# One attention kind's scores from half-height products, and a projection on rows that are normalised afterwards

## The reference, cut to what matters

```python
h = rmsnorm(x, norm1_g)                 # x * rsqrt(mean(x*x) + eps) * g, per token
proj = h @ w_in                         # 1024 x 1792, cut into aq ak av bq bk bv cu
# first kind: 4 heads, a 2-D neighbourhood, scores + relative bias, softmax, times values
# second kind: 8 query heads, 2 key/value heads, blocks of 128 queries, 3 blocks of keys
s = einsum('bnqgrd,bnkgd->bngrqk', qb, kb)      # d is 64
s = where(valid, s + alibi, -inf)               # softmax with a sink logit, times values
# third mixer: centred means over windows of 2, 4, 8, 16 tokens of cu, then a small product
x = x + concatenate([o_a, o_b, o_c]) @ w_out
# then rmsnorm, a router over 32 experts, two experts per token, and a last rmsnorm
```

## Time and profile before

| | |
|---|---|
| median of 3 runs | 747.9 us (746.43 to 748.84) |
| the profiled execution, its own time | 746.88 us |
| its span, first to last instruction | 745.0 us |
| TensorE busy | 707.8 us (95%), mean granted clock 0.986 |
| VectorE busy | 506.3 us (68%) |
| ScalarE busy | 411.1 us (55%) |
| GpSimd busy | 328.3 us (44%) |

### The profile page before, as it was taken

One profiled execution on the slowest core, in us unless ns is written; L12 is line 12 of the kernel. 1 busy time (PEld: TensorE's weight loads), 2 busy tenths in 40 slices (PEclk: granted clock), 3 DMA queues, 4 the chain that ended last, 5 costly groups with the idle time before them and its releaser, 6 DMA issues.

```text
span 745.0 us, 10230 instructions
## 1 busy us (share of the span) xinstructions
PE 707.8 (95%) x3745; PEld 522.7 (70%) x3745; DVE 506.3 (68%) x790; ACT 411.1 (55%) x619; POOL 328.3 (44%) x243
## 2 busy tenths in 40 slices
PE   6999999998898999999999899999999999999973
PEld 6888888886666665888889866666666666666631
DVE  5561110325788888613477798888888888888977
ACT  6411002224678887301122478888888888887815
POOL 3523347853578885340010144444444444443223
PEclk9999999999899999999999899999999999999998
DMA  8521111100021000915547399999999999999978
GB/s 288 154 58 58 28 57 58 56 1 1 1 58 58 0 2 1 306 34 197 187 157 255 113 347 383 381 381 382 383 387 383 390 386 382 382 386 382 393 276 342
DMA packets 62563, 157.80 MB, mean 212 GB/s; under 512 B 10184, under 2 KB 25136, under 8 KB 62512
## 3 DMA queue, kind: packets, MB, share of 16 engines
q1 hardware_dynamic: 56032, 139.72, 51.9%
q0 software_dynamic: 6336, 16.89, 6.8%
q10 hardware_dynamic: 144, 0.52, 0.2%
HBM read 142.43 MB, written 18.87 MB: 216 GB/s over the span
## 4 chain that ended last, share of the span: by engine, by line
PE 82%; DVE 6%; ACT 3%; DMA 3%; POOL 2%; issue 2%; SPq 0%; DVEq 0%; POOLq 0%
PE ps L999 8%; PE ps L1004 8%; PE ps L1007 8%; PE ps L727 6%; PE ps L728 6%; PE ps L726 6%; PE ps L882 4%; PE ps L1030 4%; PE ps L1026 4%; PE ps L884 4%; PE ps L883 4%; PE ps L1034 4%; PE ps L975 2%; POOL pswa L2030 2%; PE ps L909 2%
## 5 line engine op out<-in xcount | busy, mean ns | idle before, releaser
L1800 DVE TENSOR_TENSOR wgulo<-wgu,unit 128x2048 fp32r<-128x2048 f32 x64 | 146.3, 2287 | 27.1 <-ACT unit L1293 26.7
L1293 ACT CAST unit<-wgu 128x2048 fp32r<-128x2048 f32 x64 | 122.2, 1910 | 4.3 <-PE ps L940 2.0
L2079 POOL DMA_INDIRECT expert_rows<-ysb,idx x32 | 72.2, 2258 | 106.9 <-ACT ysb L1340 99.2
L2072 POOL DMA_INDIRECT xg<-h_rows,idx x32 | 58.8, 1839 | 73.6 <-PE ps L975 59.1
L726 PE MATMUL ps<-hThi,whi 128*128 128x512 f32 x208 | 81.4, 392 | 0.0
L728 PE MATMUL ps<-hThi,wlo 128*128 128x512 f32 x208 | 81.0, 389 | 0.0
L727 PE MATMUL ps<-hTlo,whi 128*128 128x512 f32 x208 | 80.9, 389 | 0.0
L1806 DVE TENSOR_TENSOR wdlo<-wd,unit 128x2048 fp32r<-128x2048 f32 x32 | 73.1, 2284 | 1.8 <-ACT unit L1302 1.8
L999 PE MATMUL ps<-unit,xThi 128*80 128x512 f32 x256 | 70.9, 398 | 0.8 <-ACT xThi L1317 0.8
L1004 PE MATMUL ps<-unit,xTlo 128*80 128x512 f32 x256 | 69.2, 391 | 0.0
L1007 PE MATMUL ps<-wgulo,xThi 128*80 128x512 f32 x256 | 69.1, 391 | 0.0
(11 more groups left out here) (221 smaller groups left out, 1472.9 us busy)
## 6 DMA issues: line engine op xcount, KB each, us to landing
wgu<-in_expert_w_gate SPq DMA_DIRECT2D x64, 512.0 KB, 13.0
wgu<-in_expert_w_up SPq DMA_DIRECT2D x64, 512.0 KB, 14.9
wd<-in_expert_w_down SPq DMA_DIRECT2D x32, 1024.0 KB, 16.7
y<-expert_rows SPq DMA_DIRECT2D x16, 512.0 KB, 9.9
wraw<-in_w_in SPq DMA_DIRECT2D x14, 512.0 KB, 4.0
xin<-in_x SPq DMA_DIRECT2D x8, 512.0 KB, 5.1
x<-in_x SPq DMA_DIRECT2D x8, 512.0 KB, 7.1
out<-fo SPq DMA_DIRECT2D x8, 512.0 KB, 4.1
```

Source lines behind the costliest of these rows:

```text
L1293: nc.scalar.copy(weight_unit(e, a)[:], raw_half(wgu, e, a)).then_inc(ahi_done, 1)
L1800: nc.vector.tensor_tensor(raw_half(wgulo, e, a), raw_half(wgu, e, a), weight_unit(e, a)[:].bitcast(F32), ALU.subtract).then_inc(alo_done, 1)
```

## The change

The scores of the second kind become single full-precision products over 64 rows, as those of the first kind are. So queries are kept in one unsplit tile `qs` with two heads in its two halves, and `khi`, `klo`, the split of the queries and their buffers go away. The rows are no longer normalised before the projection: the raw tiles are transposed, and the inverse roots come afterwards. They are put on diagonals (`row_scale_diagonal`, VectorE), eight products with a matrix of ones spread them over the partitions (`row_scales`, TensorE), ScalarE copies them out (`rbc`), and VectorE multiplies every projection's bank by them as it empties it. The second kind's keys are multiplied in their bank, and ScalarE makes the doubled copies from there. The first kind's query scale moves into its bias tables. The order of the first loads, of the first projection (two halves of 256 columns) and of several waits is new.

```diff
-FILL_FIRST = (3, 6, 4, 4, 8)
+FILL_FIRST = (3, 4, 2, 2)
-LAST_QUERIES = (5, 8)
+LAST_QUERIES = (4, 8)
 # sync: x 0, then weight tile 0, x 1, x 2, x 3, weight tile 1, x 4 to 7 (eight buffers);
 # ident and g1rows are now started by ScalarE, ones is a memset on GpSimd
+            sp.wait_ge(proj_out, 2 * MT)
             sp.dma_start(gbc[:], norm2_g.partition_broadcast(P)).then_inc(g_in, 16)
-            sp.wait_ge(bias_done, 4 * NA_STEPS)
-            for k in range(4):
-                load_wo(0, k)
-            sp.wait_ge(klo_done, SWA_KV)
-            sp.wait_ge(score_done, 4 * (NA_STEPS + SWA_KV))
-            for k in range(4, KT):
+            sp.wait_ge(te_ready, 1)
+            for k in range(KT):
                 load_wo(0, k)
 # tensor
+            def row_scales(n):
+                pe.wait_ge(lo_done, 13 + n)
+                for t in range(4 * n, 4 * n + 4):
+                    pe.wait_ge(diag_made, t + 1)
+                    mm = nc.tensor.matmul(ps[:, 2 + n, (t % 4) * P:(t % 4 + 1) * P], ones[:], rdiag[t][:], start=True, stop=True)
+                mm.then_inc(r_mm, 1)
-            pe.wait_ge(lo_done, 1)
-            spare(FILL_FIRST[4], 0)
-            project(0, 0)
+            project_first(0)
+            project_first(1)
             x_transposes(4)
             x_transposes(5)
             project(1, 0, range(4))
             x_transposes(6)
             x_transposes(7)
             project(1, 0, range(4, KT))
+            row_scales(0)
+            row_scales(1)
...
-                    q = qs[hh][:, i * P:(i + 1) * P]
-                    if i == 0:
-                        mm = nc.tensor.matmul(ps[:, sbank(u), 0:nk], q.bitcast(F32), kb[:, g, k0:k0 + nk], start=True, stop=True)
-                    else:
-                        nc.tensor.matmul(ps[:, sbank(u), 0:nk], q, khi[:, g, k0:k0 + nk], start=True, stop=False)
-                        mm = nc.tensor.matmul(ps[:, sbank(u), 0:nk], q, klo[:, g, k0:k0 + nk], start=False, stop=True)
+                    rows = slice((hh % 2) * HD, (hh % 2 + 1) * HD)
+                    mm = nc.tensor.matmul(ps[:, sbank(u), 0:nk], qs[rows, hh // 2, i * P:(i + 1) * P], kb[rows, g, k0:k0 + nk],
+                                          start=True, stop=True)
 # scalar: the new order of the head
+            high(0)
             square(0)
+            high(1)
+            w_high(0)
+            high(2)
+            high(3)
+            for t in range(1, NX):
+                square(t)
+            for t in range(NX, TT):
+                square(t)
+                high(t)
+            row_scales_copy(0)
+            row_scales_copy(1)
...
-                if u in LAST_QUERIES:
-                    projected(*PROJ[2 * MT - 2 + LAST_QUERIES.index(u)])
-                g = u - KHI_AT
-                if g in range(SWA_KV):
-                    nc.scalar.copy(khi[:, g, :], kb[:, g, :]).then_inc(khi_done, 1)
 # vector: a bank is emptied in one instruction, for every projection
+                    nc.vector.tensor_tensor(by_block(vT[v][:])[:, rows8], half_rows(bank), half_rows(r), ALU.mult).then_inc(proj_out, 1)
...
+                    nc.vector.scalar_tensor_tensor(out=qs[:, m - 6, cols], in0=bank, scalar=qscale[:, m - 6:m - 5], in1=r,
+                                                   op0=ALU.mult, op1=ALU.mult).then_inc(proj_out, 1)
...
                 if u in LAST_QUERIES:
-                    queries_low(2 * MT - 2 + LAST_QUERIES.index(u))
+                    projected(2 * MT - 2 + LAST_QUERIES.index(u))
 # gpsimd
-                if u in KLO_AT:
-                    gp.tensor_tensor(klo[:, g, :], kb[:, g, :], khi[:, g, :].bitcast(F32), ALU.subtract).then_inc(klo_done, 1)
```

More of the change, by code:

```diff
@@ L741, in v_transposes, with project_first @@
                     mm.then_inc(vtr_done, 1)
-            pe.wait_ge(mats_in, 32)
-            nc.tensor.transpose(ps[:, 6, 0:KT], g1rows[:], ident[0:KT, 0:KT]).then_inc(g_in, 16)
+            def project_first(half):
+                pe.wait_ge(w_split, 2)
+                pe.wait_ge(lo_done, 4 * (half + 1))
+                cols = slice(256 * half, 256 * half + 256)
+                for k in range(KT):
+                    nc.tensor.matmul(ps[:, 4, cols], whi[0][:, k, :], hThi[:, k, cols], start=(k == 0), stop=False)
+                    nc.tensor.matmul(ps[:, 4, cols], whi[0][:, k, :], hTlo[:, k, cols], start=False, stop=False)
+                    mm = nc.tensor.matmul(ps[:, 4, cols], wlo[0][:, k, :], hThi[:, k, cols], start=False, stop=(k == KT - 1))
+                if half == 1:
+                    mm.then_inc(proj_done, 1)
+            pe.wait_ge(mats_in, 16)
             for t in range(4):
-                spare(FILL_FIRST[t], 7)
+                spare(FILL_FIRST[t], 2)
                 x_transposes(t)
-            pe.wait_ge(lo_done, 1)
-            spare(FILL_FIRST[4], 0)
-            project(0, 0)
+                if t == 0:
+                    pe.wait_ge(tab_in, 16)
+                    nc.tensor.transpose(ps[:, 3, 0:KT], g1rows[:], ident[0:KT, 0:KT]).then_inc(g_in, 16)
+            project_first(0)
+            project_first(1)
             x_transposes(4)
@@ L1156, in w_high, with row_scales_copy @@
                 nc.scalar.copy(whi[0][:], wraw[0][:]).then_inc(w_split, 1)
+            def row_scales_copy(n):
+                act.wait_ge(r_mm, n + 1)
+                nc.scalar.copy(rbc[:, n * 512:(n + 1) * 512], ps[:, 2 + n, :]).then_inc(r_ready, 1)
+            high(0)
             square(0)
-            square(1)
-            high(0)
-            square(2)
             high(1)
-            square(3)
             w_high(0)
@@ L1429, in _ @@
             nc.vector.memset(pwd[:], 0.0).then_inc(zeroed, 1)
[L1431 removed]
+            for h in range(SWA_HEADS):
+                nc.vector.memset(qscale[(h % 2) * HD:(h % 2 + 1) * HD, h // 2:h // 2 + 1], query_scale(h)).then_inc(qscale_set, 1)
+            low(0)
             dve.wait_ge(g_in, 16)
[L1433 to L1434 removed]
+            nc.vector.tensor_copy(g1T[:], ps[:, 3, 0:KT]).then_inc(w_scaled, 1)
             dve.wait_ge(w_scaled, 1)
[L1436 to L1437 removed]
             w_scale(0)
             low(1)
[L1440 removed]
+            w_low(0)
             low(2)
@@ L1443, in _ @@
             w_scale(1)
-            normalise(4)
-            normalise(5)
             w_low(1)
-            normalise(6)
-            normalise(7)
+            low(4)
+            low(5)
+            dve.wait_ge(mats_in, 16)
+            for t in range(4):
+                row_scale_diagonal(t)
+            low(6)
+            low(7)
             for t in range(4, TT):
-                low(t)
+                row_scale_diagonal(t)
             w_scale(2)
+            projected(0)
+            projected(1)
@@ L1462, in _ @@
-            dve.wait_ge(const_in, 16 * 10)
+            projected(3)
+            values(0)
+            w_scale(4)
+            projected(4)
+            projected(5)
+            w_scale(5)
+            dve.wait_ge(tab_in, 16 * 4)
+            dve.wait_ge(zeroed, 3)
+            for n, tab, done in ((0, ti, ti_ready), (1, te, te_ready)):
+                if n:
+                    dve.wait_ge(ti_ready, n)
+                nc.vector.scalar_tensor_tensor(out=tab[:], in0=te[:], scalar=HD ** 0.5,
+                                               in1=namask[:, n, :].unsqueeze(1).to_broadcast([P, NA_HEADS, 3 * P]),
+                                               op0=ALU.mult, op1=ALU.subtract).then_inc(done, 1)
@@ L1463, in _ @@
+            dve.wait_ge(const_in, 16 * 9)
             nc.vector.tensor_scalar(nsink[:], nsink[:], -1.0, None, ALU.mult).then_inc(sink_set, 1)
             nc.vector.tensor_tensor(rw[:], rw[:], g2T[:].unsqueeze(2).to_broadcast([P, KT, NR]), ALU.mult).then_inc(rw_scaled, 1)
[L1465 to L1485 removed]
@@ L1487, in _ @@
+            for i in range(3, 10):
+                projected(2 * i)
+                projected(2 * i + 1)
+                if i in (3, 5):
+                    values(i // 2)
+                w_scale(i + 3)
             for g in range(2 * MT - 8, 2 * MT - 2):
-                queries_low(g)
+                projected(g)
                 if g == 2 * MT - 7:
@@ L1954, in _ @@
             gp.memset(eps_col[:], EPS).then_inc(small_done, 1)
-            pool.wait_ge(small_done, 2)
-            count = [2]
+            gp.memset(ones[:], 1.0).then_inc(small_done, 1)
+            pool.wait_ge(small_done, 3)
+            count = [3]
             def inverse_root(src, ready, n, done, t):
```

188 lines of the change are left out of this document (76 added, 112 removed).

## The result

The changed kernel takes 738.35 us (median of four, 737.93 to 739.57), the kernel before 747.94 on the same chip (746.43 to 748.84): a ratio of 0.9877, 95% interval 0.986 to 0.9893. The forecast was 738.5. The profiled execution has a span of 736.4 us and its own time is 738.25. That the total is so close is luck: two of its terms were wrong and cancelled.

The account below looks back on a forecast made before the run. TensorE, busy 95% of the span, was taken as the bound, with four engines balanced in second-kind steps. 2.2 + 4.9 + 3.4 - 1.3 = 9.2 us gained took the median from 747.9 to 738.5 us, range 733.5 to 743.5.

Parts of the forecast that it names:

- The head: Before attention: first projection at 14.0 instead of 18.43 us, less 0.3 for half-wide products and 1.95 for row scales: 2.2 us gained.
- The projections: Projection stretch: VectorE empties all 28 banks within its idle time while TensorE is the bound: 0 gained or lost.
- The start of attention: Last two query banks emptied by VectorE alone: 3.3 us less wait and 1.6 from the clock, 4.9 us gained.
- The keys' split: Around 205 us: without GpSimd's two subtractions VectorE no longer stands still; 3.4 us gained, bounds 2.0 and 4.8.
- The other scores: Second-kind steps: 0.17 us more per step for the height switch, 0.01 for products, half hidden: 1.3 us lost, bounds 0 and 2.9.
- rival (c): Attention balance: TensorE pays its 0.18 fully and more, GpSimd absorbs VectorE's saved 3.4 us: 743 to 744; chance 0.07.
- the tiling: Scores over 64 rows: the skill's up-to-twice speedup would give 0.75 for four heads; the first kind's 1.49 shows nothing of it.
- The signs that the prediction named: Included second-kind pairs of steps some 0.2 us longer and the output projection starting at about 287.7 instead of 296.9.
- (f): TensorE stays at 1.2 GHz behind the head, 5.5 us more per projection; three give 746, four 752; chance 0.04.
- (d): Larger gain: head at 11.9, first block's 1.5 counted in full, no loss by the scores; 13 us, 733.5; chance 0.06.
- After attention: Code after attention is the same and its transfers are released by its own products: moves as a whole, 0 gained.

Follow-up runs that it names:

- kernel 8: The kernel before the change, with 20 spare records ahead of each of two waiting transpose groups at the start of attention: 744.77 us.
- kernel 4: Changed kernel with the last two query banks again emptied by ScalarE and then VectorE, each in two parts: 745.49 us.
- kernel 3: Changed kernel with the keys' copies on ScalarE and subtractions on GpSimd put back, their results unused: 742.01 us.
- kernel 5: Changed kernel with second-kind scores as two half-precision products over 128 rows, operands only rounded, low parts left out: 733.77 us in one execution.
- kernel 6: Changed kernel with each second-kind score as two half-precision products over 64 rows, low parts left out: 735.82 us in one execution.
- kernel 10: Changed kernel without head spares, second-kind heads 0 and 1 scored one item earlier, heads 2 and 3 where all four were: 739.68 us.
- kernel 9: Changed kernel without head spares, second-kind heads 2 and 3 scored one item later, heads 0 and 1 where they were: 736.5 us.
- kernel 2: Changed kernel with all second-kind heads multiplying rows 0 to 63, every second head's own rows left out: 747.66 us in one execution.
- kernel 12: Kernel 9 with 7 instead of 13 router-stage spare products ahead of the second half of the tokens' ranks: 735.82 us.
- kernels 1: Changed kernel with TensorE waiting for both banks of a pair of heads before issuing the first, in second-kind steps: 737.86 us.
- kernel 7: Changed kernel without the 11 spare products of its head: 736.54 us.
- 11: Changed kernel without head spares, one rounded half-precision 64-row product per second-kind head, low parts left out: 731.86 us.

## Why the prediction was right in total, and where not

**The head: right,** 2.2 said and 2.16 measured, the first projection at 14.14 for 14.0. That the 256-column product costs half (0.12) held. The closeness is luck: in the seven profiles with the changed head the first scores come at 166.72 to 168.06, in the two with the old one at 169.93 and 170.62, so the gain is anything from 1.9 to 3.9 us. The clock rose at 7.74 to 10.71 us in those seven, and where it rose before 9 us the first projection started before 13.5. How much of the earlier start comes from raw tiles, and how much from 11 spares instead of 25, no kernel separates.

**The projections at nothing: right.** TensorE is busy 20.00 of 20 us there, with VectorE at 11.59.

**The start of attention: right,** 4.9 said, 5.06 measured, and by its two parts: the clock 1.65 (kernel 8) and the wait 3.4. Put back, the two-engine form costs 6.05 (kernel 4), 1.0 more than its removal gave; that 1.0 is not explained.

**The keys' split: right,** 3.4 said, 3.33 measured, 3.5 when put back (kernel 3).

**The other scores: the step that failed.** It said "I take half, 1.3 us lost", with 2.9 as the far bound, and 4.55 were lost. Two things were wrong in it. It counted only TensorE's time (1.49 against 1.48, and the 0.17 of the switch), and let idle time hide half. But TensorE had only 1.7 us of real waiting in three pairs, and the scores are the first link of a chain in balance: what they come later by is paid by VectorE, then by ScalarE, then by the banks. That the form of the scores costs the whole of it is shown (kernel 5). How it splits is less sure. Between kernels 5 and 6 lie 1.6 us, near the 2.0 of 12 steps at 0.17 that it had as a full price, but kernel 6 also spares TensorE 0.5 us a step, so the switch is not isolated. The other 2.9, full precision over 64 rows, it priced at 0.01 a step against kernel 5's form. Here the first bank is full later: the first two heads take 0.75 us, where the first one took 0.43 before and two took 0.45 in kernel 6. That the lateness of the first scores is the mechanism rests on VectorE's wait (0.4, 0.2 and 2.3 us for three pairs in the kernel before, kernel 5 and the changed one) and on the 0.94 us instead of 0.63 to its first operation; an experiment that gave them sooner, kernel 10, met a full bank instead, so this part is inferred and not isolated. What kernel 9 shows is the other end of the chain: 3.0 us of the stretch come back when TensorE has other work while the banks are emptied. Its own rival (c), "the balance gives back", named the place but absorbed the gain of the split there, which was in fact kept.

It also misread the tiling: "shows nothing of it" was wrong, as kernel 2 shows. The 1.49 of the first kind already had the overlap in it.

The signs that the prediction named show what the total hid: a pair of steps became 0.93 us longer and not 0.2, and the output projection started at 290.7, 3 us behind the 287.7 that it gave. Two of its rivals' prices do not follow from their own terms: three projections at 5.5 us more give about 755 and four about 761 in (f), not 746 and 752, and the terms of (d) add up to some 14 us, not 13. Neither came to bear.

**After attention: 0 said, 2.49 gained.** The code moved as a whole, but the clock did not. In the kernel before, it was at half from 406.69 for 6.83 us, in the router's stretch; in the changed one it never fell there. The stretch from the output projection to the gathered rows took 126.98, 127.16, 127.16 and 126.61 us in the four that had 6.83 us at half clock there (the kernel before and kernels 4, 9 and 12), and 125.2 to 125.7 in the changed kernel and kernels 1, 2, 3, 5 to 8 and 11, which had none there, but for kernel 3 with 3.4 us at the same place. Kernel 10 took 128.2, with 3.4 us at half clock already at 374.77. So some 1.7 of the 2.49 go with the clock. Why it falls is not settled: kernel 8 has the old code there and kept its clock, kernel 9 the new code and lost it. It may differ between executions of one kernel too, as the mean clock does (0.984 to 0.993 in those of the kernel before that ran beside kernels 1 to 4), so a single profile does not make it a property of the change. The other 0.8 us lie behind the gathered rows (321.2 before, 320.4 after), and that part took 320.0 to 321.6 us in the profiles of the changed code: no more than scatter.

So an error of -3.25 us in the scores and one of +2.49 behind attention nearly cancelled, and a forecast with partly wrong reasons came out right to 0.2 us. That is luck.

## What to carry to other kernels

Do not price a changed product by its total alone: four scores in 1.49 us either way cost 4.5 us over 12 steps. Look also at when its first result comes, at the switches around it, and at whether its banks are empty when its turn comes; which of these weighs most was not isolated here. Two 64-row products shared TensorE only where both found their banks empty; other work between such pairs gave 2.5 us of attention, and starting one early into a full bank gave nothing. And compare several profiles where a stretch scatters, and the granted clock of the two traces in every stage, the unchanged ones too, before a gain or a loss is put down to the edit.

## What the runs showed of the hardware

- Full-precision products over 64 rows in the two halves overlap almost fully: two heads in 0.75 us, each alone 0.70 (kernel 2), and, in these traces, only when issued together; head 2 of the changed kernel, whose neighbour's bank was full, took 0.66 by itself.
- Half-precision products over 64 rows overlap too: in kernel 6 the records come in twos, and four heads of two products take 0.99 us, against 1.48 over 128 rows.
- Full-precision transposes alone brought the clock up, at 11.39 us (kernel 7).
- Spares at half clock can hold back work: 26 records took 5.02 us in kernel 9, where the same 26 took 3.12 at 2.4 GHz in kernel 8. With 14 of them the ranks behind them started 1.05 us earlier (kernel 12).
